# A wider buffer of zeros; in the second mixer, conversions one a step, two low parts at later steps, and one output unit split by GpSimd into dead activation tiles

## The chip, the cores and the metric

The kernel runs on one core of one Trainium2 chip. The metric is the device time of one launch in microseconds (us); three runs of the kernel before have a median of 1670.9 us (1670.79 to 1671.87). All times below are us unless they are marked ns. PE is TensorE, DVE is VectorE, ACT is ScalarE, POOL is GpSimd, and SP is the engine that issues the loads.

## The reference, cut to what matters

Three layers run over 512 tokens of width 1024 in float32. The first is a hybrid layer, the second holds the mixer that the change touches, and the third pools over windows of tokens.

```python
def mixer_fox_nsa(h, w_in, b_f, cmp_pe, cmp_w1, cmp_w2, w_out):
    proj = h @ w_in                      # 23 column units of 128: fq, fk, fv, nq, kc, vc, ks, vs, kw, vw, gates
    ...
    o_fox = fox_attention(...)           # 8 heads of 64, softmax(q k / 8 + c_t - c_s), causal
    o_nsa = nsa_attention(...)           # per head: compressed + selected + windowed attention, gated
    return jnp.concatenate([o_fox, o_nsa], axis=-1) @ w_out

# fox_attention, per block of 128 queries:
s = jnp.einsum('bqhd,bkhd->bhqk', qi, k) * scale + ci[..., None] - c[:, :, None, :]
p = masked_softmax(s, kpos[None, :] <= t[:, None])
# nsa_attention, per block: three branches (compressed, selected "slc", window "win")
return gi[..., 0:1] * o_c + gi[..., 1:2] * o_s + gi[..., 2:3] * o_w
```

## The kernel before

**Weights.** Every projection is cut into units of 128 output columns: eight blocks of 128x128 weights, 128x1024 floats. SP loads a unit into one of four `raw` buffers. It is then split into a high part (`split_hi`, a copy rounded to the matmul's type, `whi`, semaphore `hi_done`) and a low part (`split_lo`, raw minus high, `wlo`, semaphore `lo_done`). There are two `whi` and two `wlo` buffers (`SPL = 2`), taken in turn, so that the split of unit n waits until unit n-2 has been multiplied (`unit_done`). TensorE computes each block in three matmuls of 512 columns (`three`: high x high, high x low, low x high). Normally ScalarE makes the high part and VectorE the low one. Both semaphores count units, so that units have to be split in order.

**The second mixer (`mix_b`).** Projection `in_b` has 23 units; the first eight are multiplied before, the other 15 beside the attention (`beside`, blocks per step in `BLOCKS_B`). The attention is a loop over steps k on all engines, over 48 pairs of items (`PAIRS`, `NPAIR = 48`): for each of four head pairs t there are eight pairs of the NSA branches (`nsa_at(t) = 12 t`) and four of FoX (`fox_at(t) = 12 t + 8`). What an engine does in a step is written out by hand, and the engine goes through it in that order:

- TensorE: transposes of pair k-2 (`turned`), products of pair k-3, odd pieces (`misc`: "ct", "fv", "nc"), the scores of pair k+1 (`scores`, L2425 and L2426), then blocks of `in_b`, and from step 44 on blocks of the first two output units (`early`). The scores of an item use one of two banks and wait for VectorE's maximum (`nmB`, L1915) of an earlier one.
- VectorE: reciprocals (`fcB`, L1901), two maxima (L1915), low parts of the transposed probabilities (`ptl`, L1930), sums into `outf`, conversions (`convert`, L1841), the compressed branch's sums (`cst`, L1966 to L1972), `fvs` (L1849) and `pcl`, then the low part `hlo` of an activation tile of the output projection (L1983, steps 43 to 49 and 52), then a unit of `in_b` out of PSUM (`zb`, L1408).
- ScalarE: the high parts and exponentials that these need, in the same order.
- GpSimd: the scaling of pair k-1's probabilities by `fcB` (L744, L748), small pieces of the compressed branch (`pc`, L753, L756), and the low parts of the weight units 12 to 24, one when a unit of `in_b` ended in the step before (L762). Numbers 23 and 24 are the first two units of the output projection `out_b`.

**Conversions.** A query or key row (`zb`) is split into high and low for two heads h = 0 and 1: ScalarE copies a half, then VectorE subtracts (L1841, inputs `zb` and the copy, both in SBUF). `CONV` is their list and `CONV_AT` the step of each. For FoX, `fks` and `fqs` hold the halves of `fk{t}` and `fq{t}`; after the conversion of a key, SP swaps its halves by DMA (`SWAPS`: after which load).

**Waits among these.** The piece "nc" of TensorE (L2507, first at step `nsa_at(t) + 6`) waits for `fvs` of the step before on VectorE, which stands behind the conversions of that step. The piece "ct" (L2500, step `nsa_at(t) + 4`) waits for GpSimd's `pc` (L756), which waits for VectorE's `cst` of the step before.

**The output projection.** `early` does seven of the eight blocks of its units 0 and 1. After the loop TensorE does the eighth of each, then units 2 to 7. Unit 2 would take unit 0's `whi`, so it is split when unit 0 has ended.

Of the kernel before, what the change touches and what calls it, by code (L numbers as in the profile page):

```python
# [27 lines left out]
P = 128  # L28
S = 512
# [63 lines left out]
END_LAST = {FIRST[_p] + COUNT[_p] - 1: FIRST[_p] + END_UNIT for _p in IN_HALVES}  # L93
POOL_0, POOL_1 = FIRST["pool"], FIRST["pool"] + 1

GAIN = {0: "mix_norm", 1: "ffn_norm", 2: "g00", 3: "g01", 4: "g02", 5: "g03", 6: "g10", 7: "g11",
# [27 lines left out]
def build(nc, xT, vecs, conv, sinks, w_alpha2, pe, cmp_w1, cmp_w2, weights, yT, flow=FLOW):  # L124
# [6 lines left out]
    with ctx:  # L131
# [21 lines left out]
        invc = sb("invc", [P, MAXW])  # L153
        zero = sb("zero", [P, 32], f32r)

# [223 lines left out]
        def whigh(n):  # L379
            if n == 2:  # L380
                return oh[:, 0:WU * P]
            if n == POOL_1:
                return map_pieces(alo, 8)
            if n in KEPT:
                return hhi[:, KEPT[n] * WU * P:KEPT[n] * WU * P + WU * P]
            return ahi[:, (16 + 2 * EXTRA[n]) * S:(18 + 2 * EXTRA[n]) * S] if n in EXTRA else whi[n % SPL][:, :]

        def wlow(n):
            if n == 2:
                return ol[:, 0:WU * P]  # L390
            if n == POOL_1:
                return map_pieces(alo, 12)
            if n in KEPT:
                return hlo[:, KEPT[n] * WU * P:KEPT[n] * WU * P + WU * P]
            return alo[:, (16 + 2 * EXTRA[n]) * S:(18 + 2 * EXTRA[n]) * S] if n in EXTRA else wlo[n % SPL][:, :]
# [120 lines left out]
        for t in range(4):  # L516
# [3 lines left out]
            if t == 2:  # L520
# [4 lines left out]
                CONV_AT += [nsa_at(t) - 3, nsa_at(t) - 2]  # L525
            CONV += [(f"fk{t}", h, fks[:, h, 0, :]) for h in range(2)] + [(f"fq{t}", h, fqs[:, h, :]) for h in range(2)]
            CONV_AT += [nsa_at(t) + 5, nsa_at(t) + 5, nsa_at(t) + 6, nsa_at(t) + 6]
        CONV_OF = {(name, h): i for i, (name, h, _) in enumerate(CONV)}
# [8 lines left out]
        def dest_free(name):  # L537
# [4 lines left out]
            if name[0] == "f" and t:  # L542
# [4 lines left out]
        SWAPS = [(("ks", 0), 12), (("kw", 0), 12), (("fk0", 0), 16), (("fk0", 1), 16), (("fk1", 0), 20), (("fk1", 1), 20),  # L547
                 (("ks", 1), 21), (("kw", 1), 21), (("fk2", 0), 24), (("fk2", 1), 24), (("fk3", 0), 28), (("fk3", 1), 28)]

# [111 lines left out]
        def _(pool):  # L661
# [43 lines left out]
            if has_b:  # L705
# [32 lines left out]
                for k in range(STEPS_B):  # L738
# [11 lines left out]
                    for t in range(4):  # L750
# [3 lines left out]
                        if k == nsa_at(t) + 3:  # L754
                            pool.wait_ge(B["cmp"], 5 * t + 5)
                            pool.tensor_tensor(pg, pg, over_keys(cst[:, 8:16]), ALU.mult).then_inc(B["cmp_pool"], 1)  # L756
                    for u in finished_at("in_b", k - 1) if k else []:
                        n = mix_unit + u + 2
                        pool.wait_ge(hi_done, n + 1)

                        pool.wait_ge(lo_done, n)
                        pool.tensor_tensor(wlo[n % SPL][:, :], raw[n % RAW][:, :], whi[n % SPL][:, :].bitcast(f32),  # L762
                                           ALU.subtract).then_inc(lo_done, 1)
# [47 lines left out]
        def _(act):  # L811
            def split_hi(n, i):

                act.wait_ge(raw_ready[n % RAW], raw_loaded(n) + 16 * i)
                if n in EXTRA:

# [86 lines left out]
            def gemm(p):  # L903
# [6 lines left out]
                def step(u, i):  # L910
                    split_hi(n0 + u, i)
                    evacuate(p, u - 2, i)
# [456 lines left out]
        def _(dve):  # L1369
# [131 lines left out]
            def gemm(p):  # L1501
# [4 lines left out]
                def step(u, i):  # L1506
                    split_lo(n0 + u, i)
                    evacuate(p, u - 2, i)
# [324 lines left out]
            def mix_b():  # L1833
# [62 lines left out]
                for k in range(STEPS_B):  # L1896
# [21 lines left out]
                    if k == 0:  # L1918
                        for b in range(NB):
                            r = slice(32 * b, 32 * b + 32)  # L1920
                            dve.wait_ge(B["cm_hi"], 4 + b + 1)
                            dve.tensor_tensor(vcs[r, b, :, HD:P], ps[r, 2:4, 0:HD],
                                              vcs[r, b, :, 0:HD].bitcast(f32), ALU.subtract).then_inc(B["cm_lo"], 1)
                        split_lo(FIRST[p] + 11, 0)
                    if 0 <= k - 2 < NPAIR:
# [788 lines left out]
```

## Time and profile before

| | |
|---|---|
| median of three runs | 1670.9 us |
| the profiled execution's own time | 1671.58 us |
| its span | 1669.9 us |
| second mixer and its first output units | about 630 to 860 us of the span |
| TensorE busy | 1637.7 us, 98% |
| DVE, ACT, POOL busy | 53%, 43%, 11% |

The span is the time from the first to the last instruction of the profiled execution. Its steps have no names in the profile; a step is found by the lines that run in it. In a row of the timeline the bracket is the idle time of the engine before the instruction and what ended it.

### The profile page before, as it was taken

What the parts mean: (1) busy time and instruction counts of PE and PEld (TensorE: products, weight loads), DVE (VectorE), ACT (ScalarE), POOL (GpSimd) and SP (SyncE); (2) the same over time, 40 slices, a digit from 0 to 9 for tenths busy, and PEclk for the clock granted to TensorE, in tenths of its full rate; (3) what the DMA queues carried; (4) which work ended last, traced back from release to release, by engine and by line L of the source; (5) the groups of instructions that cost most, each with busy time, mean ns of one, the idle gap of its engine ahead of it and who ended that gap; (6) DMA issues with size and microseconds to landing.
All of it is one profiled execution on the core that took longest, in us unless ns stands there. A gap on an engine that the chain in (4) does not pass through costs nothing.

```text
span 1669.9 us, 22401 instructions
## 1 busy us (share of the span) xinstructions
PE 1637.7 (98%) x8090; PEld 1351.1 (81%) x8090; DVE 883.5 (53%) x1473; ACT 710.6 (43%) x1211; POOL 176.0 (11%) x255
## 2 busy tenths in 40 slices
PE   8999999999999999999899999999999999999997
PEld 7777788888888887888777888888898888888887
DVE  5644667777743346677756544444238644444233
ACT  4555454444432226677656332232237522323221
POOL 2011000000000032445403000001001200000001
PEclk9999999999999999999999999999999999999999
DMA  5211223332333242121112233233331232333331
GB/s 180 89 39 48 81 88 101 100 100 90 97 100 91 88 129 76 39 64 52 51 51 89 89 100 97 91 100 94 95 104 61 64 100 89 100 100 89 100 101 51
DMA packets 57158, 144.87 MB, mean 87 GB/s; under 512 B 14160, under 2 KB 20976, under 8 KB 57088
## 3 DMA queue, kind: packets, MB, share of 16 engines
q1 hardware_dynamic: 55680, 141.58, 27.2%
q0 software_dynamic: 688, 1.26, 0.3%
q10 hardware_dynamic: 720, 1.10, 0.2%
q8 instruction: 44, 0.72, 0.2%
q14 instruction: 26, 0.21, 0.0%
HBM read 138.67 MB, written 2.10 MB: 84 GB/s over the span
## 4 chain that ended last, share of the span: by engine, by line
PE 93%; ACT 3%; DVE 3%; issue 1%; POOL 0%; DVEq 0%; ACTq 0%; POOLq 0%
PE ps L2027 26%; PE ps L2028 26%; PE ps L2029 26%; PE ps L2196 1%; PE ps L2128 1%; PE ps L2127 1%; PE ps L2126 1%; PE ps L2425 1%; PE ps L2478 1%; PE ps L2440 1%; PE ps L2426 1%; PE ps L2186 1%; PE ps L2599 0%; PE ps L2239 0%; PE ps L2264 0%
## 5 line engine op out<-in xcount | busy, mean ns | idle before, releaser
L2027 PE MATMUL ps<-hhi,whi 128*128 128x512 f32 x1400 | 553.1, 395 | 2.5 <-DVE wlo L1373 2.0
L2029 PE MATMUL ps<-hhi,wlo 128*128 128x512 f32 x1400 | 546.6, 390 | 0.0
L2028 PE MATMUL ps<-hlo,whi 128*128 128x512 f32 x1400 | 546.3, 390 | 0.0
L1373 DVE TENSOR_TENSOR wlo<-raw,whi 128x1024 fp32r<-128x1024 f32 x227 | 280.3, 1235 | 457.7 <-ACT whi L836 455.0
L836 ACT ACTIVATE whi<-raw 128x1024 fp32r<-128x1024 f32 x240 | 254.0, 1058 | 527.7 <-PE ps L2029 527.3
L2027 PEld LDWEIGHTS ps<-hhi,whi 128*128 128x128 f32 x1400 | 263.8, 188 | 65.4 <-issue 8.2
L2029 PEld LDWEIGHTS ps<-hhi,wlo 128*128 128x128 f32 x1400 | 263.4, 188 | 56.1
L2028 PEld LDWEIGHTS ps<-hlo,whi 128*128 128x128 f32 x1400 | 263.8, 188 | 53.3 <-issue 1.2
L2029 PE MATMUL ps<-ahi,wlo 128*128 128x512 f32 x432 | 170.6, 395 | 0.0
L2027 PE MATMUL ps<-ahi,whi 128*128 128x512 f32 x432 | 170.6, 395 | 0.0
L2028 PE MATMUL ps<-alo,whi 128*128 128x512 f32 x432 | 170.6, 395 | 0.0
L901 ACT ACTIVATE ahi<-gated 128x512 f32 (+1 forms) x66 | 41.8, 633 | 148.2 <-DVE gated L1496 148.2
L1467 DVE TENSOR_TENSOR pre<-ps,rstd 128x512 f32<-128x512 f32 x132 | 90.1, 684 | 22.5 <-ACT rstd L1057 14.8
L2028 PEld LDWEIGHTS ps<-alo,whi 128*128 128x128 f32 x432 | 81.1, 188 | 19.8
L2027 PEld LDWEIGHTS ps<-ahi,whi 128*128 128x128 f32 x432 | 81.1, 188 | 19.7
L2029 PEld LDWEIGHTS ps<-ahi,wlo 128*128 128x128 f32 x432 | 81.1, 188 | 19.6
L1498 DVE TENSOR_TENSOR alo<-gated,ahi 128x512 f32 (+1 forms) x66 | 45.7, 693 | 59.3 <-ACT ahi L901 59.3
L1279 ACT ACTIVATE pth<-ps 128x128 fp32r<-128x128 f32 (+3 forms) x96 | 36.7, 433 | 39.7 <-PE ps L2440 39.1
L1930 DVE TENSOR_TENSOR ptl<-ps,pth 128x128 fp32r<-128x128 f32 (+3 forms) x96 | 42.9, 486 | 11.6 <-ACT pth L1279 11.4
L711 POOL DMA_DIRECT2D cw<-cmp_w x4 | 3.4, 854 | 424.2 <-PE ps L2029 424.2
L890 ACT ACTIVATE cvt<-pre,convw 128x512 f32<-128x512 f32 x44 | 35.5, 809 | 28.8 <-DVE pre L1467 28.8
L1285 ACT ACTIVATE pB<-pB,nmB 128x512 f32<-128x512 f32 (+3 forms) x80 | 44.2, 557 | 6.7 <-DVE nmB L1915 6.5
(373 smaller groups left out, 2051.3 us busy)
## 6 DMA issues: line engine op xcount, KB each, us to landing
raw<-w_up_b SPq DMA_DIRECT2D x88, 512.0 KB, 3.4
raw<-w_up_a SPq DMA_DIRECT2D x44, 512.0 KB, 3.4
raw<-w_in_b SPq DMA_DIRECT2D x23, 512.0 KB, 3.5
raw<-w_in_a SPq DMA_DIRECT2D x19, 512.0 KB, 3.5
raw<-w_down_b SPq DMA_DIRECT2D x16, 512.0 KB, 3.5
raw<-w_out_a SPq DMA_DIRECT2D x8, 512.0 KB, 3.4
raw<-w_down_a SPq DMA_DIRECT2D x8, 512.0 KB, 3.5
raw<-w_out_b SPq DMA_DIRECT2D x8, 512.0 KB, 3.6
```

The costliest lines, as they stand in the source:

```text
L836: act.activation(whigh(n), raw_of(n), ACT.Copy).then_inc(hi_done, 1)
L890: act.activation(cvt[:, s, :], pre[:, s, :], ACT.Identity, bias=convw[:, bass.ds(3 * 2 * KF + c + fi, 1)], scale=convw[:, bass.ds(2 * 2 * ...
L901: act.activation(tile(ahi, f + fi), gated[:, :], ACT.Copy).then_inc(k["ahi"], 1)
L1279: act.activation(pth[:, j % 2, 0:n, s % 2, :], ps[:, 2 + s % 2, 0:n * P].rearrange("p (j q) -> p j q", q=P), ACT.Copy).then_inc(B["hi"], 1)
L1285: act.activation(ptile(s)[:, 0:w], ptile(s)[:, 0:w], ACT.Exp, scale=-1.0, bias=nmB[:, s:s + 1], accum_out=smB[:, s:s + 1]).then_inc(B["p"], 1)
L1373: dve.tensor_tensor(wlow(n), raw_of(n), whigh(n).bitcast(f32), ALU.subtract).then_inc(lo_done, 1)
L1467: dve.tensor_tensor(pre[:, u % 2, :], ps[:, u % 4, :], rstd[:, :], ALU.mult).then_inc(evac[p], 1)
L1498: dve.tensor_tensor(tile(alo, f + fi), gated[:, :], tile(ahi, f + fi).bitcast(f32), ALU.subtract).then_inc(k["alo"], 1)
L1930: dve.tensor_tensor(ptl[:, j % 2, 0:n, s % 2, :], ps[:, 2 + s % 2, 0:n * P].rearrange("p (j q) -> p j q", q=P), pth[:, j % 2, 0:n, s % 2, ...
L2027: pe_.matmul(out, wh, hi, start=start, stop=False)
L2028: pe_.matmul(out, wh, lo, start=False, stop=False)
L2029: return pe_.matmul(out, wl, hi, start=False, stop=stop)
```

## The change

- `zero`, a constant buffer in front of the larger tiles, grows from 32 to 64 columns of 4 bytes. Only its column 0 is read. Its fill on GpSimd writes 64 columns, and all buffers allocated after it stand 128 bytes further on in each partition.
- Conversions of head pair t = 3: before, `fk3` halves 0 and 1 at step 41 and `fq3` halves 0 and 1 at step 42. Now `fq3` at 39 and 40, `fk3` at 41 and 42. SP swaps `fk3` after load 27 in place of 28, because load 28 now waits for a later low part.
- Two low parts: VectorE's `split_lo` of unit 11 moves from step 0 to step 1, behind the maxima. GpSimd's low part of unit 24 (output unit 1) moves from step 41 to step 43.
- Output unit 2 (`OUT_2`) is split by GpSimd into tiles of `ahi` that are dead there: the high part at step 45, the low part at step 47. ScalarE and VectorE split it no more. Unit 3 waits for both semaphores; unit 4 waits for unit 0 alone.

```diff
+OUT_2 = FIRST["out_b"] + 2
-        zero = sb("zero", [P, 32], f32r)
+        zero = sb("zero", [P, 64], f32r)
@@ whigh(n), and wlow(n) with ahi[:, 5 * S:7 * S]
+            if n == OUT_2:
+                return ahi[:, 3 * S:5 * S]
@@ the list of conversions
-            CONV += [(f"fk{t}", h, fks[:, h, 0, :]) for h in range(2)] + [(f"fq{t}", h, fqs[:, h, :]) for h in range(2)]
-            CONV_AT += [nsa_at(t) + 5, nsa_at(t) + 5, nsa_at(t) + 6, nsa_at(t) + 6]
+            CONV += fk_halves + fq_halves if t < 3 else fq_halves + fk_halves
+            CONV_AT += [nsa_at(t) + a for a in ((5, 5, 6, 6) if t < 3 else (3, 4, 5, 6))]
@@ SWAPS
-                 (("ks", 1), 21), (("kw", 1), 21), (("fk2", 0), 24), (("fk2", 1), 24), (("fk3", 0), 28), (("fk3", 1), 28)]
+                 (("ks", 1), 21), (("kw", 1), 21), (("fk2", 0), 24), (("fk2", 1), 24), (("fk3", 0), 27), (("fk3", 1), 27)]
@@ GpSimd, loop of mix_b
-                    for u in finished_at("in_b", k - 1) if k else []:
+                    if k == NPAIR - 3:
+                        pool.wait_ge(raw_ready[OUT_2 % RAW], raw_loaded(OUT_2))
+                        pool.wait_ge(B["conv_lo"], CONV_OF["q3", 1] + 1)
+                        pool.wait_ge(hi_done, OUT_2)
+                        pool.tensor_copy(whigh(OUT_2), raw[OUT_2 % RAW][:, :]).then_inc(hi_done, 1)
+                    if k == NPAIR - 1:
+                        pool.wait_ge(hi_done, OUT_2 + 1)
+                        pool.wait_ge(lo_done, OUT_2)
+                        pool.tensor_tensor(wlow(OUT_2), raw[OUT_2 % RAW][:, :], whigh(OUT_2).bitcast(f32), ALU.subtract
+                                           ).then_inc(lo_done, 1)
+                    last_unit = [COUNT["in_b"] - 1] if k == NPAIR - 5 else []
+                    for u in [u for u in finished_at("in_b", k - 1) if u < COUNT["in_b"] - 1] + last_unit if k else []:
@@ ScalarE, split_hi
-                if n in EXTRA:
+                if n == OUT_2 + 1:
+                    act.wait_ge(hi_done, n)
+                if n == OUT_2 + 2:
+
+                    act.wait_ge(unit_done, n - 3)
+                elif n in EXTRA:
@@ ScalarE, step(u, i) of gemm
-                    split_hi(n0 + u, i)
+                    if n0 + u != OUT_2:
+                        split_hi(n0 + u, i)
@@ VectorE, step(u, i) of gemm
-                    split_lo(n0 + u, i)
+                    if n0 + u == OUT_2 + 1:
+                        dve.wait_ge(lo_done, n0 + u)
+                    if n0 + u != OUT_2:
+                        split_lo(n0 + u, i)
@@ VectorE, loop of mix_b, behind `if k == 0:`
+                    if k == 1:
                         split_lo(FIRST[p] + 11, 0)
```

Three places show how rows move. The line numbers of the changed kernel are higher by 6 to 27; the forms tell the same rows. The first is VectorE at steps 0 and 1 of the mixer, from the last piece of the compressed branch's values (`vcs`) on. Before:

```order
L1922 TENSOR_TENSOR vcs<-ps,vcs 32x2x64 x4
L1373 TENSOR_TENSOR wlo<-raw,whi 128x1024
L1955 SCALAR_TENSOR_TENSOR pc<-distC,ps 128x256
L1901 RECIPROCAL fcB<-smB 128x2
L1915 ISA pB,nmB<-ps,distB 128x128
L1915 ISA nmB 128x1
L1915 ISA pB,nmB<-ps,distB 128x128
L1915 ISA nmB 128x1
```

and now:

```order
L1948 TENSOR_TENSOR vcs<-ps,vcs 32x2x64 x4
L1982 SCALAR_TENSOR_TENSOR pc<-distC,ps 128x256
L1927 RECIPROCAL fcB<-smB 128x2
L1941 ISA pB,nmB<-ps,distB 128x128
L1941 ISA nmB 128x1
L1941 ISA pB,nmB<-ps,distB 128x128
L1941 ISA nmB 128x1
L1396 TENSOR_TENSOR wlo<-raw,whi 128x1024
```

The low part of unit 11 (`wlo<-raw,whi`) stood ahead of step 1's `pc`, reciprocal and two maxima, and now stands behind them. The second is VectorE at steps 41 and 42, from step 41's `ptl` on. Before:

```order
L1930 TENSOR_TENSOR ptl<-ps,pth 128x2x128 x2
L1841 SCALAR_TENSOR_TENSOR fks<-zb,fks 64x512 x2
L1849 TENSOR_TENSOR fvs<-ps,fvs 128x8x64
L1901 RECIPROCAL fcB<-smB 128x2
L1915 ISA pB,nmB<-ps,distB 128x512
L1915 ISA nmB 128x1
L1915 ISA pB,nmB<-ps,distB 128x512
L1915 ISA nmB 128x1
L1930 TENSOR_TENSOR ptl<-ps,pth 128x3x128 x2
L1841 SCALAR_TENSOR_TENSOR fqs<-zb,fqs 64x512 x2
```

and now:

```order
L1957 TENSOR_TENSOR ptl<-ps,pth 128x2x128 x2
L1867 SCALAR_TENSOR_TENSOR fks<-zb,fks 64x512
L1875 TENSOR_TENSOR fvs<-ps,fvs 128x8x64
L1927 RECIPROCAL fcB<-smB 128x2
L1941 ISA pB,nmB<-ps,distB 128x512
L1941 ISA nmB 128x1
L1941 ISA pB,nmB<-ps,distB 128x512
L1941 ISA nmB 128x1
L1957 TENSOR_TENSOR ptl<-ps,pth 128x3x128 x2
L1867 SCALAR_TENSOR_TENSOR fks<-zb,fks 64x512
```

Step 41 keeps one conversion ahead of `fvs` and step 42 keeps one ahead of step 43; the two `fqs` rows that are missing here stand at steps 39 (between `outf` and `cst`) and 40 (ahead of `pcl`). The third is GpSimd from the scaling ahead of step 41's low part on. Before:

```order
L748 TENSOR_SCALAR pB<-pB,fcB,gates 128x384 x2
L762 TENSOR_TENSOR wlo<-raw,whi 128x1024
L748 TENSOR_SCALAR pB<-pB,fcB,gates 128x384
L748 TENSOR_SCALAR sq<-sq,fcB,gates 128x384
L748 TENSOR_SCALAR pB<-pB,fcB,gates 128x512 x4
L744 TENSOR_SCALAR pB<-pB,fcB,invc 128x128
L744 TENSOR_SCALAR sq<-sq,fcB,invc 128x256
L744 TENSOR_SCALAR pB<-pB,fcB,invc 128x384
L744 TENSOR_SCALAR pB<-pB,fcB,invc 128x512
L744 TENSOR_SCALAR pB<-pB,fcB,invc 128x384
L744 TENSOR_SCALAR pB<-pB,fcB,invc 128x512
L744 TENSOR_SCALAR pB<-pB,fcB,invc 128x128
```

and now, from step 43 on:

```order
L754 TENSOR_SCALAR pB<-pB,fcB,gates 128x512 x2
L779 TENSOR_TENSOR wlo<-raw,whi 128x1024
L754 TENSOR_SCALAR pB<-pB,fcB,gates 128x512 x2
L750 TENSOR_SCALAR pB<-pB,fcB,invc 128x128
L750 TENSOR_SCALAR sq<-sq,fcB,invc 128x256
L767 CAST ahi<-raw 128x1024
L750 TENSOR_SCALAR pB<-pB,fcB,invc 128x384
L750 TENSOR_SCALAR pB<-pB,fcB,invc 128x512
L750 TENSOR_SCALAR pB<-pB,fcB,invc 128x384
L750 TENSOR_SCALAR pB<-pB,fcB,invc 128x512
L771 TENSOR_TENSOR ahi<-raw,ahi 128x1024
L750 TENSOR_SCALAR pB<-pB,fcB,invc 128x128
```

The low part of output unit 1 moved down by two steps (past the two 128x384 rows and two 128x512 rows), and two rows for output unit 2 are new: a copy behind the first FoX pair's scaling and a subtraction behind the third's.

## Rows read from the trace of the kernel before

**Rows 1.** The page: TensorE's busy time, share of the span, instructions.

```profile
PE 1637.7 (98%) x8090; PEld 1351.1 (81%) x8090; DVE 883.5 (53%) x1473; ACT 710.6 (43%) x1211; POOL 176.0 (11%) x255
```

**Rows 2.** Waits of TensorE, whole span: total us, times, longest us.

```profile
PE ps L2425 <- DVE nmB L1915: 7.4, 16, 2.3
```

**Rows 3.** Stretches of 2 us: busy time of each engine, granted clock (PEclk).

```profile
648.00:650.00 2.00, 1.75 (x9) 1.31 (x10) 1.49 (x8) 1.80 (x9) 2.00 (x5) 0.59 0.63 145
650.00:652.00 2.00, 2.00 (x8) 1.66 (x8) 0.90 (x5) 0.80 (x4) 1.14 (x3) 0.55 0.59 117
...
822.00:824.00 2.00, 2.00 (x10) 1.80 (x10) 1.43 (x3) 1.98 (x6) 0.10 (x1) 0.61 0.70 192
824.00:826.00 2.00, 2.00 (x10) 1.65 (x10) 1.94 (x6) 1.75 (x5) 0.91 (x2) 0.53 0.01 4
...
828.00:830.00 2.00, 0.62 (x6) 0.41 (x4) 1.61 (x7) 1.95 (x5) 0.19 (x1) 1.00 0.00 0
...
856.00:858.00 2.00, 2.00 (x8) 1.54 (x7) 1.83 (x2) 1.03 (x3) 0.00 (x0) 0.65 0.77 201
858.00:860.00 2.00, 2.00 (x6) 1.61 (x5) 0.00 (x0) 0.00 (x0) 0.00 (x0) 0.50 0.79 219
```

**Rows 4.** Timeline, steps 0 to 2: start, duration, instruction, idle before it.

```profile
645.76 1.22 DVE L1373 TENSOR_TENSOR wlo<-raw,whi 128x1024 fp32r<-128x1024 f32 x1 [0.72 <-ACT whi L836]
...
647.02 0.42 DVE L1955 SCALAR_TENSOR_TENSOR pc<-distC,ps 128x256 f32<-128x256 f32 x1
...
647.86 0.36 PE L2425 MATMUL ps<-kst,qst 128*128 128x256 f32 x1 [2.27 <-DVE nmB L1915]
...
649.36 0.55 PE L2425 MATMUL ps<-kst,qst 128*128 128x256 f32 x1 [0.25 <-DVE nmB L1915]
```

**Rows 5.** Timeline, steps 39 to 42.

```profile
808.33 0.69 DVE L1939 TENSOR_TENSOR outf<-ps,sq 64x512 f32<-64x512 f32 x1 [1.28 <-ACT sq L1299]
...
810.83 0.41 PE L2500 MATMUL ps<-ident,pc 128*128 128x128 f32 x2 [0.24 <-POOL pc L756]
...
816.24 2.38 POOL L762 TENSOR_TENSOR wlo<-raw,whi 128x1024 fp32r<-128x1024 f32 x1
...
817.44 2.45 DVE L1841 SCALAR_TENSOR_TENSOR fks<-zb,fks 64x512 fp32r<-64x512 f32 x2 [0.97 <-ACT fks L1228]
...
819.92 0.69 DVE L1849 TENSOR_TENSOR fvs<-ps,fvs 128x512 fp32r<-128x512 f32 x1
...
820.67 0.49 PE L2507 MATMUL ps<-csr,esel 128*128 128x512 f32 x1 [2.41 <-DVE fvs L1849]
```

**Rows 6.** Timeline, steps 42 to 44.

```profile
823.39 1.40 DVE L1841 SCALAR_TENSOR_TENSOR fqs<-zb,fqs 64x512 fp32r<-64x512 f32 x2 [0.57 <-ACT fqs L1228]
...
830.05 0.41 PE L2425 MATMUL ps<-fks,fqs 128*128 128x384 f32 x1 [1.43 <-DVE nmB L1915]
```

**Rows 7.** Timeline, step 47: GpSimd's scaling and VectorE's split of an activation tile.

```profile
840.44 1.42 POOL L744 TENSOR_SCALAR pB<-pB,fcB,invc 128x384 f32<-128x384 f32 x2 [1.98 <-DVE fcB L1901]
...
844.51 0.69 DVE L1983 TENSOR_TENSOR hlo<-outf,hhi 128x512 fp32r<-128x512 f32 x1
```

**Rows 8.** Timeline, the third output unit.

```profile
854.10 1.23 DVE L1373 TENSOR_TENSOR wlo<-raw,whi 128x1024 fp32r<-128x1024 f32 x1 [1.79 <-ACT whi L836]
...
855.38 0.50 PE L2027 MATMUL ps<-hhi,whi 128*128 128x512 f32 x1 [1.86 <-DVE wlo L1373]
```

**Rows 9.** Timeline, a GpSimd copy beside a two-input VectorE instruction.

```profile
1289.95 1.22 DVE L1373 TENSOR_TENSOR alo<-raw,ahi 128x1024 fp32r<-128x1024 f32 x1
1290.26 1.82 POOL L772 CAST whi<-raw 128x1024 fp32r<-128x1024 f32 x1 [10.44 <-DVE sq L1383]
```

**Rows 10.** Group of GpSimd by form: count, busy us, mean ns.

```profile
L679 POOL MEMSET zero<- 128x32 f32 x1 | 0.1, 125 | 0.1
```

**Rows 11.** Groups of TensorE by form.

```profile
L2027 PE MATMUL ps<-hhi,whi 128*128 128x512 f32 x1400 | 553.1, 395 | 2.5 <-DVE wlo L1373 2.0 <-DVE hlo L1983 0.5
...
L2027 PE MATMUL ps<-ahi,whi 128*128 128x512 f32 x432 | 170.6, 395 | 0.0
```

More of the change, by code:

```diff
@@ L390, in wlow @@
                 return ol[:, 0:WU * P]
+            if n == OUT_2:
+                return ahi[:, 5 * S:7 * S]
             if n == POOL_1:
@@ L525, in build @@
                 CONV_AT += [nsa_at(t) - 3, nsa_at(t) - 2]
-            CONV += [(f"fk{t}", h, fks[:, h, 0, :]) for h in range(2)] + [(f"fq{t}", h, fqs[:, h, :]) for h in range(2)]
-            CONV_AT += [nsa_at(t) + 5, nsa_at(t) + 5, nsa_at(t) + 6, nsa_at(t) + 6]
+            fk_halves, fq_halves = [(f"fk{t}", h, fks[:, h, 0, :]) for h in range(2)], [(f"fq{t}", h, fqs[:, h, :]) for h in range(2)]
+            CONV += fk_halves + fq_halves if t < 3 else fq_halves + fk_halves
+            CONV_AT += [nsa_at(t) + a for a in ((5, 5, 6, 6) if t < 3 else (3, 4, 5, 6))]
         CONV_OF = {(name, h): i for i, (name, h, _) in enumerate(CONV)}
```

## The prediction

> **What bounds the kernel now.** I read the page first: TensorE is busy for 98% of the span [rows 1], so a change that leaves its work alone can only win its idle time, and time in which it ran slowly. The changed kernel issues the same matmuls. The list of TensorE's waits has one large entry, the wait of the scores for VectorE's maxima: 7.4 us in 16 waits, the longest 2.3 [rows 2]. The table of stretches then says what a wait costs besides itself. The granted clock is at its upper level (2.4 GHz) nearly everywhere, and lies between 0.50 and 0.65 in three places, at 648 to 652, 822 to 826 and 856 to 860 [rows 3]. Each follows one of the three long idle times: 2.27 us before the scores at 647.86 [rows 4], 2.41 before the "nc" piece at 820.67 [rows 5] and 1.86 before the third output unit at 855.38 [rows 8]. The idle 1.43 us that ends at 830.05 [rows 6] was not followed by a fall: its stretch shows 1.00 [rows 3]. The lost clock is 2 x (0.41 + 0.45) = 1.7 us in the first place, 2 x (0.39 + 0.47) = 1.7 in the second and 2 x (0.35 + 0.50) = 1.7 in the third, where the level fallen to is 1.2 GHz. The timeline around the three places shows who is late, and the change touches all three.
>
> **Place 1, steps 0 and 1.** VectorE waits 0.72 for ScalarE's high part, subtracts for 1.22, and only then comes to `pc` at 647.02, behind which stand the maxima that TensorE waits for [rows 4]. With the low part behind the maxima, `pc` starts 0.72 + 1.22 = 1.9 earlier, and the idle 2.27 falls to about 0.4. But the low part now stands ahead of step 2's maxima. It can start at about 646.1, may be held by GpSimd's scaling for up to one instruction, ends at 647.3 to 647.8, and a sum and a reciprocal (0.5 together, by the 0.42 of `pc`) follow. The scores that began at 649.36 begin at 648.4 to 648.9. Gain 0.5 to 1.0; I take 0.8, between the two. Whether the clock still falls is open: TensorE idles twice for shorter times instead of once for 2.27, but does little between. If it does not fall, TensorE's work behind 649.36 gains another 1.2 us (the part of the slow stretch in which it never waited). If it does, some 0.3 of the gain is lost, since more work falls into the slow stretch. I take the fall as staying: 0.8 - 0.3 = 0.5 in all, with 0.2 and 2.2 as ends. The unit itself (11) is wanted far later than either place, at step 4.
>
> **Place 2, steps 39 to 44.** Three terms.
> - Step 39, a loss. VectorE's new `fqs` row stands between `outf` (808.33, ends 809.02) and `cst`. From `cst` the chain goes to GpSimd's `pc` and to TensorE's "ct" piece, which already waited 0.24 for it [rows 5]. So the row costs its whole length: 0.7, half of the 1.40 that two take alone [rows 6]. The 1.28 that VectorE idles there lies ahead of `outf`, waits for ScalarE, and cannot cover it. The `fqs` row at step 40 costs nothing: its cover is VectorE's idle time before the next `zb`; without that cover it would cost another 0.7.
> - Step 41, a gain. `fvs` stands behind two conversions that take 2.45 instead of 1.40, the time in which GpSimd's low part (816.24 to 818.62) runs [rows 5, 6]. Now one conversion is left and GpSimd's low part has moved: `fvs` follows at 817.44 + 0.7 = 818.1 instead of 819.92, 1.8 earlier. TensorE arrives 0.7 late from step 39 and still idles for about 0.6 in place of 2.41. Net of both terms: 1.1.
> - Step 42, a gain. One conversion (0.7) leaves VectorE's chain ahead of step 43's maxima. Behind these stand `outf`, `hhi`, `hlo` and step 44's maxima, for which TensorE waited 1.43 [rows 6]. VectorE is the bound there, so 0.7 arrives in full. The slow clock of this place is gone with its idle time, but that buys nothing more, because TensorE then only arrives sooner at the same wait. Here lies a danger: it could idle some 1.6 us before 830.05, between the 1.43 that left the clock alone and the 1.86 that did not.
>
> Sum of place 2: 1.8, with 0.4 (the clock falls at step 44, 1.4 of the 1.7 lost behind it) and 2.1 as ends. GpSimd's later low part of output unit 1 runs behind step 43's scaling, from about 826 to 828.5 on the old time scale; early block 0, the first to need it, comes at 831. SP's load 28 waits for it, wanted tens of us later. The swap of `fk3` no longer has that load in front of it and its first half is asked for no later than before.
>
> **Place 3, output unit 2.** After unit 0 has ended, ScalarE copies and VectorE subtracts (854.10, 1.23 long), and TensorE idles for 1.86 [rows 8]. With both parts made during steps 45 and 47, it goes from unit 1 straight into unit 2. Nothing takes the wait's place: unit 3 needs unit 1 gone and has all of unit 2's multiplication, over 5 us, as cover for its 2.3 us of splitting. Gain 1.86 and the 1.7 of clock, all of it in a stretch where TensorE never waited: 3.5, with 1.8 (idle gone, clock falls elsewhere) and 3.6 as ends.
>
> What GpSimd pays: a copy (the nearest row has 1.82, next to a VectorE instruction with two SBUF inputs that began before it [rows 9]; below it, a subtraction's 2.38 [rows 5] is the upper bound, and nothing the lower) and a subtraction of 2.38. It idles before each scaling, 1.98 before the one at 840.44 [rows 7], so its own order holds. What it can do to VectorE: the conversions at 817.44 were held while its subtraction ran [rows 5], and its copy was held in turn [rows 9]. Rows say, then, that a VectorE instruction with two inputs in SBUF waits for a GpSimd instruction that runs. The Trainium skill says the same in SBUF — State Buffer, "SBUF: two separate sides": the two engines share a port pair as an exclusive lock for a whole instruction. By that rule the trace agrees, with 1.05 us lost in one place; it speaks against giving GpSimd three long instructions between steps 43 and 47, where VectorE splits an activation tile (`hlo`, two inputs in SBUF) in every step. By the rows: step 47's scaling ends at 841.86, the subtraction would end at 844.3, and `hlo` starts at 844.51 [rows 7]. So 0.2 us separates them; I take no collision and 0.3 as the likely most.
>
> **The rest.** 128 bytes of shift: matmuls with their inputs at other places (`hhi` and `ahi`) have the same mean, 395 ns [rows 11], so zero. The fill of `zero` took 125 ns [rows 10] and at most doubles, 0.1 at the start; I take zero.
>
> **Sum.** 0.5 + 1.8 + 3.5 = 5.8. The profiled execution took 1671.58 with a span of 1669.9; it becomes 1665.8 with 1664.1. The median of the runs stands 0.7 below the profiled one, so I forecast 1665.1.
>
> **The rivals.**
> - *The clock also stays up at place 1.* For it: 2.27 becomes two shorter idle times. Against: little work lies between them. 1.6 more: 1663.5.
> - *The clock falls where the stalls were only shortened* (place 1 and step 44, or behind an idle time that I have not seen). For it: falls followed idle times only little longer than those I leave. 1.4 to 1.7 back: 1666.7.
> - *Only place 3 pays.* The terms of VectorE are eaten by what is late next (ScalarE's exponentials, the "ct" chain). For it: VectorE waits for ScalarE before most of these rows. 3.5 or less: 1667.4 and up, near the bound of no change.
> - *The lock decides, and the kernel is slower.* If GpSimd's long instructions at steps 43, 45 and 47 each catch `hlo`, VectorE loses up to 2.4 + 1.8 + 2.4 = 6.6 us, TensorE waits for `hlo` in its early blocks, and its clock falls twice more (3.4). 10.0 against 5.8: 1675. It decides from a collision of all three on; one alone costs 2.4 + 1.7 and leaves 1.7 of gain. Against it: the gaps above; for it: one is only 0.2 wide.
>
> **How the numbers follow.** Forecast 0.40, clock up at place 1 0.22, clock falls elsewhere 0.18, only place 3 0.13, lock 0.07. 0.2% of the time is 3.3 us, about what a measurement tells from no change. The first three give a gain above it, and of the fourth a third: faster 0.84, same 0.11 (most of the fourth and a part of the lock's single collisions), slower 0.05. The range takes in the second case's full 1.7 (1663.2) and reaches up to the fourth's 1667.6; the lock and the worst of the fourth are left out.
>
> **What the profile would show.** Right: idle before the scores at 647 below 0.6; `fks` rows of 0.69 at step 41; "nc" with an idle time near 0.6; no idle before unit 2 and a clock of 1.00 through 860; a "ct" wait of about 0.9 at step 40. Wrong: `hlo` rows longer than 0.8 at steps 43 to 48, a granted clock near 0.5 within 826 to 834, or TensorE waiting for ScalarE where it waited for VectorE.

## The result and the profile after

The changed kernel takes 1655.92 us (median of 6 runs, 1655.0 to 1656.6), the kernel before 1671.82 beside it: ratio 0.9907, interval 0.9894 to 0.9919. It is faster by 15.5 to 16 us, where 5.8 were forecast; the time lies 7 us below the range. The profiled execution took 1656.2 with a span of 1654.5.

The page, the waits of TensorE and two-microsecond stretches of the kernel after, the counterparts of [rows 1 to 3]:

```profile
PE 1626.6 (98%) x8090; PEld 1350.5 (82%) x8090; DVE 878.7 (53%) x1472; ACT 709.3 (43%) x1210; POOL 181.4 (11%) x257
```

```profile
PE ps L2452 <- DVE nmB L1941: 5.8, 16, 1.4
...
PE ps L2527 <- POOL pc L762: 0.8, 1, 0.8
```

```profile
640.00:642.00 2.00, 1.62 (x13) 1.50 (x14) 1.84 (x10) 1.76 (x6) 0.51 (x1) 0.94 0.00 0
642.00:644.00 2.00, 1.68 (x7) 1.12 (x7) 2.00 (x8) 0.75 (x4) 2.00 (x3) 0.50 0.00 0
644.00:646.00 2.00, 2.00 (x8) 1.71 (x7) 1.18 (x6) 1.65 (x7) 1.34 (x4) 0.50 0.70 161
646.00:648.00 2.00, 2.00 (x8) 1.60 (x7) 0.18 (x2) 0.27 (x2) 0.65 (x2) 0.50 0.55 109
648.00:650.00 2.00, 2.00 (x11) 1.83 (x11) 1.21 (x5) 1.20 (x6) 0.53 (x1) 0.85 0.00 0
...
816.00:818.00 2.00, 2.00 (x13) 1.41 (x14) 1.30 (x5) 1.95 (x6) 0.52 (x1) 1.00 0.30 71
...
852.00:854.00 2.00, 2.00 (x10) 1.66 (x9) 0.47 (x1) 1.09 (x2) 0.00 (x0) 1.00 0.69 219
```

TensorE issues the same 8090 matmuls, yet its busy time fell by 11.1 us (1637.7 to 1626.6). Shorter waits cannot do that, and 3.4 us less of slow clock (6.8 between 600 and 900 us in place of 10.2) make 1.7 of it. So some matmuls themselves got quicker. The granted clock is at its upper level at the second and third place. At the first it fell although the idle time went, and stayed down twice as long (6.8 us, 641.8 to 648.6).

The groups of TensorE by form show where the busy time went. The kernel before, with the two forms beside those of [rows 11]:

```profile
L2029 PE MATMUL ps<-hhi,wlo 128*128 128x512 f32 x1400 | 546.6, 390 | 0.0
...
L2029 PE MATMUL ps<-ahi,wlo 128*128 128x512 f32 x432 | 170.6, 395 | 0.0
```

The kernel after:

```profile
L2054 PE MATMUL ps<-hhi,whi 128*128 128x512 f32 x1392 | 549.4, 395 | 0.6 <-DVE hlo L2010 0.4 <-DVE wlo L1396 0.2
L2056 PE MATMUL ps<-hhi,wlo 128*128 128x512 f32 x1392 | 543.0, 390 | 0.0
...
L2054 PE MATMUL ps<-ahi,whi 128*128 128x512 f32 x432 | 168.0, 389 | 0.0
...
L2056 PE MATMUL ps<-ahi,wlo 128*128 128x512 f32 x432 | 168.0, 389 | 0.0
```

Every matmul of 512 columns that streams `ahi` (the name in front of the comma; the one behind it holds the weights) lost 6 ns of 395; those with `hhi` kept theirs. The prediction compared `hhi,whi` with `ahi,whi`, both 395. But `hhi,whi` is the form that comes first behind a wait or behind other work (0.50 us long at [rows 8]), and its mean stands 5 ns above the two other forms of `hhi`. The durations of the kernel before show it (shortest, median and longest, in ns):

```profile
L2027 PE MATMUL ps<-hhi,whi x1400: 387/389/799, 8.5 to 1534.6; 128*128 128x512 f32 x175
L2027 PE MATMUL ps<-ahi,whi x432: 392/394/398, 456.6 to 1624.2; 128*128 128x512 f32 x144
```

The medians are 5 ns apart where the means are equal. Like compared with like (`hhi,wlo` 390, `ahi,wlo` 395), the groups would have shown that matmuls with `ahi` were slow.

The timeline gives the same as the distance between starts. Down projection, before and after (the same kind of stretch, not the same matmuls):

```profile
1136.35 0.40 PE L2027 MATMUL ps<-ahi,whi 128*128 128x512 f32 x1
...
1137.52 0.39 PE L2029 MATMUL ps<-ahi,wlo 128*128 128x512 f32 x1
```

```profile
1126.05 0.39 PE L2054 MATMUL ps<-ahi,whi 128*128 128x512 f32 x1
...
1127.18 0.39 PE L2056 MATMUL ps<-ahi,wlo 128*128 128x512 f32 x1
```

In each pair the second start comes five matmuls behind the first: 1.17 / 5 = 0.234 us before, 1.13 / 5 = 0.226 after.

Matching the matmuls of both traces one by one by their order, the start of the same matmul is earlier in the kernel after by this much: 0.4 us in the first mixer's output projection, 4.3 at the first place, 4.4 behind it, 3.8 behind the ct piece of step 40, 5.6 at the nc piece, 6.2 at step 44, 9.9 behind output unit 2, 15.4 at the end. So 5.6 us came in the second mixer, where the prediction looked for all of its 5.8, and the rest in the projections that read `oh`, `ol`, `ahi` and `alo`.

The rows at the three places in the kernel after. Step 1, for [rows 4]:

```profile
641.65 0.45 PE L2452 MATMUL ps<-kst,qst 128*128 128x256 f32 x1 [0.38 <-DVE nmB L1941]
...
643.06 0.91 PE L2467 MATMUL ps<-ident,pB 128*128 128x128 f32 x2 [0.32 <-POOL pB L754]
```

Steps 40 to 44, for [rows 5, 6]:

```profile
806.98 0.41 PE L2527 MATMUL ps<-ident,pc 128*128 128x128 f32 x2 [0.80 <-POOL pc L762]
...
813.62 0.69 DVE L1867 SCALAR_TENSOR_TENSOR fks<-zb,fks 64x512 fp32r<-64x512 f32 x1 [0.96 <-ACT fks L1251]
...
815.09 0.49 PE L2534 MATMUL ps<-csr,esel 128*128 128x512 f32 x1 [0.64 <-DVE fvs L1875]
...
819.56 0.30 PE L2452 MATMUL ps<-fks,fqs 128*128 128x128 f32 x1 [0.48 <-DVE nmB L1941]
...
823.88 0.41 PE L2452 MATMUL ps<-fks,fqs 128*128 128x384 f32 x1 [1.43 <-DVE nmB L1941]
```

Steps 45 to 47, GpSimd's work on output unit 2, for [rows 7, 9]:

```profile
827.12 1.04 POOL L767 CAST ahi<-raw 128x1024 fp32r<-128x1024 f32 x1
...
835.64 2.40 POOL L771 TENSOR_TENSOR ahi<-raw,ahi 128x1024 fp32r<-128x1024 f32 x1
...
838.32 0.69 DVE L2010 TENSOR_TENSOR hlo<-outf,hhi 128x512 fp32r<-128x512 f32 x1
```

### The profile page after: what moved, and what is told of

Same layout as the page of the kernel before. It is cut to its first block, busy times and chain, and to the rows that moved or that the text cites. A ratio compares the mean times of both kernels' runs of the same rounds, so it can differ in the third digit from the quotient of the medians.

```text
span 1654.5 us, 22402 instructions
## 1 busy us (share of the span) xinstructions
PE 1626.6 (98%) x8090; PEld 1350.5 (82%) x8090; DVE 878.7 (53%) x1472; ACT 709.3 (43%) x1210; POOL 181.4 (11%) x257
## 4 chain that ended last, share of the span: by engine, by line
PE 93%; ACT 3%; DVE 2%; issue 1%; POOL 0%; DVEq 0%; ACTq 0%; POOLq 0%
PE ps L2054 26%; PE ps L2055 26%; PE ps L2056 26%; PE ps L2155 1%; PE ps L2153 1%; PE ps L2154 1%; PE ps L2223 1%; PE ps L2467 1%; PE ps L2452 1%; PE ps L2505 1%; PE ps L2453 1%; PE ps L2213 1%; PE ps L2626 0%; PE ps L2291 0%; PE ps L2266 0%
## 5 line engine op out<-in xcount | busy, mean ns | idle before, releaser
L1396 DVE TENSOR_TENSOR wlo<-raw,whi 128x1024 fp32r<-128x1024 f32 x226 | 276.8, 1225 | 444.6 <-ACT whi L858 441.6
L1412 DVE TENSOR_TENSOR sq<-sq 128x512 f32<-128x512 f32 x42 | 28.9, 688 | 35.6 <-ACT sq L896 25.8
```

The costliest lines, as they stand in the source:

```text
L1396: dve.tensor_tensor(wlow(n), raw_of(n), whigh(n).bitcast(f32), ALU.subtract).then_inc(lo_done, 1)
L1412: dve.tensor_tensor(sumsq[:, :], sumsq[:, :], sq[:, m % 2, :], ALU.add).then_inc(sq_used, 1)
```

## The experiments

**The two parts of the change apart.** The first run has nothing but the wider `zero`, the second everything else, both as written in the diff of the change.

```diff
-        zero = sb("zero", [P, 32], f32r)
+        zero = sb("zero", [P, 64], f32r)
```

*zeros_only.* 

> The kernel before with the wider buffer of zeros alone (all buffers behind it 128 bytes further on). Theory A (the place of buffers is the term that I took as zero): the pitch of the three matmuls with ahi and alo falls from 0.233 to 0.227 us, which over some 1,650 matmuls of 512 columns is 9 to 10 us: ratio 0.994. Theory B (the steps of the mixer gave it all, the buffer nothing): ratio 1.000.

Measured 1661.39 (1660.83 to 1661.92), ratio 0.9941 [0.9925, 0.9958]: 9.7 us faster.

*rest_only.* 

> The changed kernel with the buffer of zeros back at 32 columns. Theory A: only the mixer's three places pay, 5.6 us: ratio 0.9966, and the pitch with ahi is 0.233 again. Theory B: ratio 0.9907 as for the whole change.

Measured 1666.06 (1665.34 to 1666.84), ratio 0.9970 [0.9958, 0.9983]: 5.0 us faster. The two add up to 14.7, nearly the whole. B is refuted.

**Where the buffers stand.** `front_pad` puts an unused buffer ahead of all others, so that everything moves by 128 bytes together; `front_pad_zeros` has both edits.

```diff
+        pad = sb("pad", [P, 32])
         raw = [sb(f"raw{i}", [P, WU * P]) for i in range(RAW)]
```

*front_pad.* 

> The kernel before with an unused buffer of 128 bytes ahead of all others, so that the weights' buffers move together with the activations. Theory A1 (relative: a matmul is slow when weights and moving columns start at different distances modulo 256 bytes): nothing changes, ratio 1.000. Theory A2 (absolute: the start of the moving columns modulo 256 bytes alone decides): ahi gains 10 us, but hhi, until now fast, loses 6 ns in each of some 4,200 matmuls, 26 us: ratio 1.010. Theory A3 (any shift of ahi by 128 bytes does it): ratio 0.994.

*front_pad_zeros.* 

> The kernel before with both, the unused buffer ahead of all and the wider buffer of zeros, so that ahi stands 256 bytes further on and the weights 128. Theory A1 (relative): as the buffer of zeros alone, ratio 0.994. Theory A2 (absolute): ahi stays slow and hhi becomes slow, ratio 1.016. Theory A3: ahi is 256 bytes further on, which is no shift of 128: ratio 1.000.

Measured 1671.1, ratio 0.9999 [0.9989, 1.0009], and 1661.85, ratio 0.9945 [0.9928, 0.9961]. In `front_pad` the `ahi` buffers stand at 128, where A2 wants them, and `hhi` at 0, and nothing is won or lost. In `front_pad_zeros` they stand at 0 again, as in the slow kernel, but so do the weights, and all is won. It is the distance that counts, not the place.

**Which distance.** `zero` with 48, 96 and 128 columns: 64, 256 and 384 bytes of shift in all.

*zeros_48.* 

> The kernel before with `zero` 48 columns wide: a shift of 64 bytes, so that ahi stands 192 bytes off the weights, modulo 256. Theory A1 with a unit of 256 bytes and no finer one: as slow as before, 1671.0, ratio 1.000, mean 395 ns. If the rule is one of 64-byte lines, any multiple of 64 would be alike and 128 could not have differed from 0, so this is not expected. If the cost grows with the distance (128 the worst, 64 and 192 half of it): 1666.2, ratio 0.997, mean 392.

*zeros_96.* 

> The kernel before with `zero` 96 columns wide: everything behind it (ahi, alo, oh, ol and the mixers' buffers) moves by 256 bytes, and so stands again 128 bytes off the weight buffers, modulo 256. Theory A1 (what counts is where the moving operand stands against the weights, modulo 256 bytes): nothing is gained, 1671.0 us, ratio 1.000, and the matmuls with ahi keep their mean of 395 ns. Rival A3' (any wider `zero` helps, because the fill or the bank layout behind it changes): 1661.4 as in the run with 64 columns, ratio 0.994.

*zeros_128.* 

> The kernel before with `zero` 128 columns wide: a shift of 384 bytes, so that ahi and the weights are level modulo 256 again, but not modulo 512 as they were with 64 columns (there the distance was 149 x 512 bytes, here it is 149.5). Theory A1 with modulo 256: 1661.4, ratio 0.994, mean 389. If the unit is 512 bytes: 1671.0, ratio 1.000, mean 395.

Measured: 48 columns 1669.22, ratio 0.9988 [0.9979, 0.9998]; 96 columns 1671.03, ratio 0.9999 [0.9989, 1.0009]; 128 columns 1662.21, ratio 0.9947 [0.993, 0.9963]. 96 columns refute A3: more zeros, and the gain is gone. A unit of 512 bytes is refuted too, since 384 bytes of shift serve as well as 128. A distance of 192 modulo 256 (48 columns) is as slow as 128 for the matmuls of 512 columns: those with `ahi` have 394 ns. That kernel is still 2.1 us faster than the one before, for another reason: its 528 matmuls of 256 columns with `ahi` or `alo` start some 3.1 ns closer together (`ahi,hhi` from 283 to 280 ns), which is 1.6 us, and the 168 of 512 columns with `hhi` or `hlo` moving and the weights in `ahi`, `alo`, `oh` or `ol`, there at a distance of 64, gain 3.7 ns each, 0.6 us.

**The converse.** An unused buffer behind `x` sets `hhi` and `hlo` off the weights and, with all that follows, brings `ahi` level with them.

```diff
         x = sb("x", [P, KD * S])
+        pad = sb("pad", [P, 32])
```

*pad_behind_x.* 

> The kernel before with an unused buffer of 128 bytes behind x: hhi and hlo now stand 128 bytes off the weights, ahi, alo, oh and ol level with them. Theory A1 asks for a loss here that is larger than the gain: some 4,200 matmuls with hhi or hlo by 6 ns are 25 us lost, some 1,500 with ahi, alo, oh or ol by 6 ns are 9 us won, so about 1687, ratio 1.010, with hhi,wlo going from 390 to 395 ns and ahi,wlo from 395 to 389. Rival (only ahi and its like are sensitive, whatever the reason): 1661.4, ratio 0.994.

Measured 1683.28 (1682.18 to 1684.38), ratio 1.0072 [1.0055, 1.0089]: 12 us slower. The groups of TensorE by form of this kernel:

```profile
L2030 PE MATMUL ps<-hhi,wlo 128*128 128x512 f32 x1400 | 553.5, 395 | 0.0
...
L2030 PE MATMUL ps<-ahi,wlo 128*128 128x512 f32 x432 | 168.1, 389 | 0.0
```

Both groups changed sides: 395 where 390 was, 389 where 395 was. Only the size was off, since 6 ns is too much for `hhi`. The distances from each start to the next, averaged over the matmuls of 512 columns in which it is below 0.4, in us:

| moving, weights (count before) | before | after | pad_behind_x |
|---|---|---|---|
| hhi or hlo, whi or wlo (4200) | 0.2285 | 0.2284 | 0.2337 |
| ahi or alo, whi or wlo (1320) | 0.2333 | 0.2267 | 0.2268 |
| oh or ol, whi or wlo (192) | 0.2345 | 0.2299 | 0.2300 |
| hhi or hlo, ahi, alo, oh or ol (168) | 0.2350 | 0.2295 | 0.2350 |

The last row holds the weights elsewhere: `hhi` keeps its place in the first two kernels and its matmuls become quicker, and in `pad_behind_x` `ahi` stands level with `whi` but 128 off `hhi`, and these matmuls are slow again. So what counts is the distance between the two operands of the matmul itself, not that to `whi` and `wlo`, which stand together in every run.

For the changed kernel: 1320 x 6.6 ns + 192 x 4.6 + 168 x 5.5 = 8.7 + 0.9 + 0.9 = 10.5 us, against 9.7 measured with `zeros_only`; some 0.7 go to the matmuls of 256 columns, which became some 1.3 ns slower each. For `pad_behind_x`: 4200 x 5.2 = 21.8 lost, 8.6 + 0.9 = 9.5 won, net 12.3, against 12.0 measured.

**Place 1.** The low part of unit 11 back where it was, `if k == 1:` to `if k == 0:` in the changed kernel.

*place1_undone.* 

> The changed kernel, with the low part of weight unit 11 back ahead of the maxima of step 0 (k == 0 in place of k == 1). Changed kernel: 1655.9. In its trace the idle time of 2.27 us is gone, but the clock stays at its lower level for 6.8 us there and not for 3.4. Theory: that took back nearly all, so undoing this part costs only about 0.2: 1656.1, with the idle time of 2.2 us back and one fall of 3.4 us. Rival (the part is worth its idle time, and the longer fall belongs to something else): 1657.8, and a fall of 6.8 us that stays.

Measured 1657.24 (1656.22 to 1657.54), ratio 0.9917 [0.99, 0.9934]. Its profiled execution has the same span as the changed kernel, 1654.5. The timeline of TensorE:

```profile
643.62 0.55 PE L2452 MATMUL ps<-kst,qst 128*128 128x256 f32 x1 [2.27 <-DVE nmB L1941]
```

The idle time is back, and the clock was down for 3.4 us rather than 6.8, so the two cancel in this pair of traces. The longer stretch does not belong to the moved low part, however: it is there in `zeros_only`, `front_pad`, `front_pad_zeros`, `zeros_96` and `pad_behind_x` too, which all have the low part where it was, and it is missing in `place3_undone`, `low_twice`, `conv_undone_swap_27` and `fq_step_40`, which have it moved. The medians say 1.3 in favour of the move, with intervals that overlap. Worth 0 to 1.3; more can't be said.

**Place 2.** The conversions of the last group back at steps 41 and 42.

```diff
-            CONV += fk_halves + fq_halves if t < 3 else fq_halves + fk_halves
-            CONV_AT += [nsa_at(t) + a for a in ((5, 5, 6, 6) if t < 3 else (3, 4, 5, 6))]
+            CONV += fk_halves + fq_halves
+            CONV_AT += [nsa_at(t) + a for a in (5, 5, 6, 6)]
...
-                 ... (("fk3", 0), 27), (("fk3", 1), 27)]
+                 ... (("fk3", 0), 28), (("fk3", 1), 28)]
```

*conversions_undone.* 

> The changed kernel with the conversions of the second mixer's last group back at steps 41 and 42, two a step (and the swap of the second key half back at 28), while GpSimd's low part of the last mixer unit stays at its new step. Theory, from the terms of the prediction: the 0.6 lost at step 39 comes back, the conversions at step 41 are no longer held by GpSimd (1.4 for two, not 2.45), so the idle time before the nc piece is some 1.3, and the 1.43 of step 44 is back: about 0.7 slower than the changed kernel, 1656.6; if one of these idle times makes the clock fall, 1.7 more, 1658.3. Rival (the hold by GpSimd was no cost, and the conversions' own place gave everything): idle time of 2.4 and a fall, 1659.3.

Measured 1665.58 (1664.8 to 1666.14), ratio 0.9965 [0.9952, 0.9977]: both theories missed. TensorE's timeline and SP's of this kernel:

```profile
815.46 0.50 PE L2534 MATMUL ps<-csr,esel 128*128 128x512 f32 x1 [1.36 <-DVE fvs L1875]
...
829.42 0.45 PE L2452 MATMUL ps<-fks,fqs 128*128 128x128 f32 x1 [8.84 <-DMA fks<-fks]
```

```profile
821.36 2.35 POOL L779 TENSOR_TENSOR wlo<-raw,whi 128x1024 fp32r<-128x1024 f32 x1
```

```profile
823.74 0.33 SPq L639 DMA_DIRECT2D raw<-w_out_b  x1
824.11 0.47 SPq L614 DMA_DIRECT2D fks<-fks  x1
```

The scores of `fks` wait 8.84 us for the swap. On SP's queue the swap stands behind a load that needs its `raw` buffer free, that is, GpSimd's low part, which now ends at 823.71. So the moved low part needs the number 27 of the swap; without it the kernel loses some 9 us. The next run keeps 27 and undoes the conversions alone.

*conv_undone_swap_27.* 

> As conversions_undone, but the swap of fk3 keeps its new number 27, ahead of load 28 on SP's queue. Theory: the 8.8 us that the scores of fks waited were the swap behind load 28, which stands behind GpSimd's moved low part; they are gone, and what is left is the price of the conversions' places: 0.6 back at step 39, idle time of about 1.3 before the nc piece and 1.4 at step 44, 0.7 to 1.0 in all: 1656.6 to 1656.9, or 1658.3 if the clock falls after one of them. Rival (the swap is late by itself, since its second half is converted only at step 41 or 42): the wait for the transfer of fks stays over 4 us, 1662 or more.

Measured 1656.91 (1656.27 to 1658.6), ratio 0.9917 [0.9899, 0.9935]. The wait for the swap is gone, so it was the queue. TensorE's timeline:

```profile
805.73 0.41 PE L2527 MATMUL ps<-ident,pc 128*128 128x128 f32 x2 [0.18 <-POOL pc L762]
814.55 0.50 PE L2534 MATMUL ps<-csr,esel 128*128 128x512 f32 x1 [1.36 <-DVE fvs L1875]
...
823.93 0.41 PE L2452 MATMUL ps<-fks,fqs 128*128 128x384 f32 x1 [1.43 <-DVE nmB L1941]
```

With GpSimd's low part out of the way, but two conversions at step 41, the idle time of 2.41 [rows 5] is 1.36: the hold by GpSimd was 1.05, the second conversion 0.7. Matched one by one, this kernel gains 0.6 on the changed one at step 39, and gives back 0.7 at step 41 and 0.6 behind it: the conversions' new places are worth 0.7 net in this pair of traces, 1.0 by the medians, whose intervals overlap.

*fq_step_40.* In the changed kernel `(3, 4, 5, 6)` becomes `(4, 4, 5, 6)`. 

> The changed kernel with the first conversion of fq3 at step 40 beside the second, and none at step 39. Theory by the prediction's step (the row at step 39 delays the ct piece by its length, and the two conversions at step 40 are covered by VectorE's idle time before zb): the ct piece waits 0.2 in place of 0.8, and 0.6 is won, 1655.3. Rival (TensorE only comes sooner to the nc piece, whose time VectorE's fvs at step 41 sets): the 0.6 is idle time there, 1655.9.

Measured 1655.43 (1654.13 to 1656.08), ratio 0.9906 [0.9888, 0.9924]. TensorE's timeline:

```profile
804.85 0.41 PE L2527 MATMUL ps<-ident,pc 128*128 128x128 f32 x2 [0.20 <-POOL pc L762]
...
813.04 0.49 PE L2534 MATMUL ps<-csr,esel 128*128 128x512 f32 x1 [0.43 <-DVE fvs L1875]
```

The ct piece waits 0.20 instead of 0.80, and the nc piece does not wait longer for it (0.43, was 0.64). The matched starts gain 0.6 at the ct piece and keep 0.5 of it behind the nc piece, so the trace is for the first theory. It is the best kernel by its median, but 0.5 us is less than the runs can tell.

**Place 3.** Output unit 2 split as before, by ScalarE and VectorE; the rest of the change stays.

```diff
-            if n == OUT_2:
-                return ahi[:, 3 * S:5 * S]
...
-                    if k == NPAIR - 3:
...
-                        pool.tensor_copy(whigh(OUT_2), raw[OUT_2 % RAW][:, :]).then_inc(hi_done, 1)
...
-                    if n0 + u != OUT_2:
-                        split_lo(n0 + u, i)
+                    split_lo(n0 + u, i)
```

*place3_undone.* 

> The changed kernel with output unit 2 split as before, by ScalarE and VectorE behind unit 0. Theory: idle time of 1.9 before unit 2 and a fall of the clock that costs 1.7 come back, 3.7 by the traces: 1659.6. Rival (with the other stalls gone the clock has more work behind it and stays up): 1657.8.

Measured 1658.71 (1657.26 to 1659.98), ratio 0.9924 [0.9908, 0.9941], 2.8 slower than the changed kernel. Its TensorE waits 1.84 before unit 2:

```profile
848.33 0.50 PE L2031 MATMUL ps<-hhi,whi 128*128 128x512 f32 x1 [1.84 <-DVE wlo L1376]
```

The stretch of 850 to 852 then shows a clock of 0.50. Matched with the changed kernel, the loss over this place alone is 3.8, as the theory says (3.7); the whole execution loses only 2.9, because 0.6 was won at place 1 and 0.2 ahead of it. The intervals of the two ratios overlap a little, the times of their runs don't (1655.0 to 1656.6, 1657.26 to 1659.98).

**The lock.** In the changed kernel GpSimd makes the low part of unit 2 twice.

```diff
                     if k == NPAIR - 1:
...
+                        pool.tensor_tensor(wlow(OUT_2), raw[OUT_2 % RAW][:, :], whigh(OUT_2).bitcast(f32), ALU.subtract
+                                           ).then_inc(twice, 1)
+                        pool.wait_ge(twice, 1)
                         pool.tensor_tensor(wlow(OUT_2), raw[OUT_2 % RAW][:, :], whigh(OUT_2).bitcast(f32), ALU.subtract
```

*low_twice.* 

> The changed kernel, in which GpSimd makes the low part of output unit 2 twice, one behind the other, at the last step but one. In the changed kernel its 2.40 us end 0.28 before VectorE's hlo starts (838.04, 838.32); twice as long it would end at 840.4. Theory (a VectorE instruction with two inputs in SBUF waits until the running GpSimd instruction ends, and GpSimd's next one waits for it in turn): hlo is held for up to 2.1 us, TensorE, which waited 0.2 for it, idles some 2.2, and the clock may fall (1.7): 1658.0 to 1659.7. Rival (the two share the bandwidth, both get slower but nobody is held): hlo takes 1.0 to 1.4 in place of 0.69, 1656.4.

Measured 1658.58 (1658.51 to 1659.03), ratio 0.9925 [0.9909, 0.9942], 2.7 slower than the changed kernel. The timeline:

```profile
837.29 2.36 POOL L774 TENSOR_TENSOR ahi<-raw,ahi 128x1024 fp32r<-128x1024 f32 x1
837.48 2.71 DVE L2013 TENSOR_TENSOR hlo<-outf,hhi 128x512 fp32r<-128x512 f32 x1
...
840.25 0.50 PE L2057 MATMUL ps<-hhi,whi 128*128 128x512 f32 x1 [2.21 <-DVE hlo L2013]
```

`hlo` begins 0.19 behind the second subtraction, takes 2.71 instead of 0.69, and ends 0.54 behind it: it was held to about the end of GpSimd's instruction and then ran (0.54 where it takes 0.69 alone; GpSimd's times are rough). GpSimd's own instruction kept its 2.4. The rival, sharing with 1.0 to 1.4 for `hlo`, is refuted; the hold is shown. The prediction's kind of price for one collision stands, a wait of 2.2 of TensorE and a fall of the clock, but its size was 4.1 (2.4 + 1.7), and measured are 2.7 by the medians and 3.2 by the matched starts.

## Why the prediction was wrong, by its steps

- **"128 bytes of shift: ... so zero."** This step failed: the term put at zero measured 9.7 us, which covers the whole miss of 9.2 (1665.1 forecast, 1655.92 measured). The rows that it rested on [rows 11] compared two groups whose equal means hid two effects: one group is raised by what it waits for, the other by its place in memory. And even two truly equal means at other places would only have said that those two distances are alike, not that a new one is. In its place the runs show the start of the moving operand against the weights, modulo 256 bytes.
- **Place 1, 0.5.** The traces show 0.15, undoing it 0 to 1.3. The idle time fell from 2.27 to 0.38 and 0.32 as said. That the clock would fall anyway was right, that it stays down longer was not foreseen, and happens in kernels without this part of the change too.
- **Place 2, 1.8.** 1.7 by the matched starts. Step 39 lost 0.6 (0.7 said), the nc piece came 1.8 sooner (1.8 said) and waits 0.64 (0.6 said), step 42 brought 0.6 (0.7 said). The idle time of 1.43 before step 44 stayed what it was, and the clock did not fall behind it.
- **Place 3, 3.5.** 3.7 in the traces, with the wait and the slow stretch gone; 2.8 by the medians of the undone kernel. The traces of `zeros_96`, `front_pad` and `front_pad_zeros` have the wait without a fall of the clock, so some executions lose less there; that this makes the difference was not shown.
- **The lock.** GpSimd's subtraction ended 0.28 before `hlo`, where 0.2 was forecast; no collision. Its copy took 1.04, not 1.82; no VectorE instruction with two inputs in SBUF ran beside it.
- **Sum.** 5.8 was forecast for what is now `rest_only`; that ran 5.0 faster, at 1666.06, and the forecast was 1665.1. The mixer's sum was right to 0.8 us by the medians; its matched starts show 5.6 behind output unit 2. Where the rest went was not shown; the clock of the kernel before, which does not fall at each place in every execution, is a candidate. None of the rivals explains the result, since all of them left the shift at zero.

## What to carry to other kernels

A change in the size of a small buffer moves every buffer behind it. For matmuls of 512 columns of this type, list where the moving operand and the weights of the most frequent matmuls start, modulo 256 bytes, before and after, and compare forms that wait equally (not the first of a group with another) to see whether a pair is slow. Matmuls of 256 columns go the other way here, so count both. Where a low part that frees a buffer is moved later, look at what stands behind that buffer's load on the DMA queue: here a swap 9 us too late.

## What the runs showed of the hardware

- A matmul of 128x512 (f32 weights and moving operand of 4 bytes an element) starts 0.227 us after the one before where both operands start level modulo 256 bytes, and 0.232 to 0.234 at a distance of 128 or 192. A distance of 64 was seen only in the 168 matmuls named with `zeros_48`: their mean is 0.2313, between 0.2298 level (`zeros_only`) and 0.2350 at 128. A matmul of 256 columns with `ahi` is slowest where both are level: its start and the next lie 0.120 apart level, 0.119 at 128 and 0.116 at 192 (means over the 384 with weights in `hhi` or `hlo`). What in the chip makes that difference was not tried: only these distances, and no other type or PSUM layout.
- The same wait is not followed by the same clock in each execution. `zeros_96` has the wait of [rows 8] unchanged:

```profile
856.15 0.50 PE L2027 MATMUL ps<-hhi,whi 128*128 128x512 f32 x1 [1.86 <-DVE wlo L1373]
```

```profile
856.00:858.00 2.00, 1.85 (x8) 1.53 (x9) 1.84 (x4) 1.79 (x3) 0.00 (x0) 1.00 0.38 86
858.00:860.00 2.00, 2.00 (x11) 1.63 (x10) 0.68 (x2) 0.00 (x0) 0.00 (x0) 1.00 0.82 254
```

The clock stays at its upper level here, where before it fell to 0.50. In the eight profiled kernels that keep all three long waits, the clock was down for 6.8 to 13.6 us between 600 and 900 us, 10.7 on average; in the five with only the first of them left, or none, for 3.4 or 6.8. Each place's 1.7 is thus a price with a chance, except at the first place, where the clock fell in all 16 traces.
- In the kernel after, the clock fell at 641.8, behind an idle time of only 0.38. From 600 to 640 TensorE had been busy throughout, but from 638.9 on with short matmuls, of 32 columns and then of 128. So at the first place it is not the idle time alone that brings the fall, and what does was not settled.
